# Moving layer 3's modulation slabs into layer 2's gated linear attention, with one pair of banks for the level planes

## What is computed

```python
for i in range(4):
    m_lat = (cond_lat @ mod_w[i] + mod_b[i]).reshape(1, 6, 1, 1024)     # and m_ctx alike
    h = x * (1 + m[1]) + m[0]
    y = mixer_i(h)                    # i == 2: bidirectional gated linear attention
    x = layer_norm(alpha * x + m[2] * y)
    h = x * (1 + m[4]) + m[3]
    x = layer_norm(alpha * x + m[5] * conv_ffn(h))
# the gated linear attention, per head and direction, in chunks of tokens:
#   o = q*exp(b) @ s + tril(sum_d q_i k_j exp(b_i - b_j)) @ v ;  s = s*exp(b_last) + (k*exp(b_last-b))^T v
```

## Time and profile before

| | |
|---|---|
| median of 3 runs | 2703.88 us (2703.25 to 2704.19) |
| the profiled execution's own time | 2701.32 us |
| its span, first to last instruction | 2699.5 us |
| mean granted TensorE clock, of 1 | 0.965 |
| TensorE matmuls busy | 2489.7 us (92%) |
| VectorE busy | 1499.6 us (56%) |
| ScalarE busy | 1172.0 us (43%) |
| GpSimd busy | 444.0 us (16%) |
| DMA | 310.43 MB, mean 115 GB/s |

### The profile page before, as it was taken

One profiled execution on the slowest core, in us unless ns is written; L12 is line 12 of the kernel. 1 busy time (PEld: TensorE's weight loads), 2 busy tenths in 40 slices (PEclk: granted clock), 3 DMA queues, 4 the chain that ended last, 5 costly groups with the idle time before them and its releaser, 6 DMA issues.

```text
span 2699.5 us, 37949 instructions
## 1 busy us (share of the span) xinstructions
PE 2489.7 (92%) x14922; PEld 2001.1 (74%) x14922; DVE 1499.6 (56%) x2244; ACT 1172.0 (43%) x2196; POOL 444.0 (16%) x443
## 2 busy tenths in 40 slices
PE   6999899999998899999999986788999999888997
PEld 3755877778888477777788875568777788856997
DVE  2465655553534857455434378867545434466874
ACT  3365533332422755333325344445333324256663
POOL 0000311110200012111012146623111002101111
PEclk8999999999999999999999997889999999999998
DMA  8602266653232013666433210013656434512663
GB/s 249 212 17 89 85 186 184 183 166 95 68 109 71 1 48 119 186 183 184 123 88 103 79 40 1 1 40 93 181 180 187 141 98 92 139 40 67 191 177 106
DMA packets 500561, 310.43 MB, mean 115 GB/s; under 512 B 24144, under 2 KB 499328, under 8 KB 500384
## 3 DMA queue, kind: packets, MB, share of 16 engines
q1 hardware_dynamic: 498048, 307.39, 38.8%
q10 hardware_dynamic: 2336, 0.61, 0.1%
HBM read 306.91 MB, written 1.05 MB: 114 GB/s over the span
## 4 chain that ended last, share of the span: by engine, by line
PE 79%; DVE 9%; ACT 5%; issue 4%; DMA 2%; POOL 0%; SPq 0%; ACTq 0%; DVEq 0%; POOLq 0%
PE bank L1463 69%; PE bank L1515 3%; PE bank L1642 1%; DMA slab_raw<-in_mod_w 1%; ACT p L641 1%; DVE stat L1105 1%; PE bank L1655 1%; PE bank L1683 1%; DMA slab_raw<-in_a_w_o 1%; DVE masked L1212 1%; DVE scores L1218 1%; DVE slab_lo L886 1%; ACT pt L653 1%; ACT slab_hi L460 1%; ACT hb L475 1%
## 5 line engine op out<-in xcount | busy, mean ns | idle before, releaser
L1463 PE MATMUL bank<-h_hi,slab_hi 128*128 128x512 f32 (+1 forms) x2416 | 857.6, 355 | 39.0 <-DVE slab_lo L886 26.0
L886 DVE TENSOR_TENSOR slab_lo<-slab_raw,slab_hi 128x1024 fp32r<-128x1024 f32 (+1 forms) x388 | 550.5, 1421 | 584.3 <-ACT slab_hi L460 583.2
L1463 PE MATMUL bank<-h_lo,slab_hi 128*128 128x512 f32 (+1 forms) x2416 | 835.1, 346 | 0.0
L1463 PE MATMUL bank<-h_hi,slab_lo 128*128 128x512 f32 (+1 forms) x2416 | 834.8, 346 | 0.0
L460 ACT ACTIVATE slab_hi<-slab_raw 128x1024 fp32r<-128x1024 f32 (+1 forms) x388 | 401.5, 1036 | 535.5 <-PE bank L1463 289.0
L1463 PEld LDWEIGHTS bank<-h_hi,slab_hi 128*128 128x128 f32 x2416 | 463.7, 192 | 147.1 <-issue 89.9
L1463 PEld LDWEIGHTS bank<-h_hi,slab_lo 128*128 128x128 f32 x2416 | 463.4, 192 | 55.7
L1463 PEld LDWEIGHTS bank<-h_lo,slab_hi 128*128 128x128 f32 x2416 | 464.1, 192 | 50.5 <-issue 0.8
L855 ACT ACTIVATE conv<-bank,prm 128x512 f32<-128x512 f32 (+1 forms) x176 | 127.2, 723 | 356.9 <-PE bank L1463 356.8
L1463 PE MATMUL bank<-g_hi,slab_hi 128*128 128x512 f32 (+1 forms) x770 | 269.3, 350 | 2.1 <-ACT res_t L511 2.1
L1463 PE MATMUL bank<-g_hi,slab_lo 128*128 128x512 f32 (+1 forms) x770 | 267.2, 347 | 0.0
(11 more groups left out here) (209 smaller groups left out, 3076.0 us busy)
## 6 DMA issues: line engine op xcount, KB each, us to landing
slab_raw<-in_mod_w SPq DMA_DIRECT2D x192, 512.0 KB, 4.6
slab_raw<-in_ffn_w_up SPq DMA_DIRECT2D x176, 512.0 KB, 4.7
slab_raw<-in_ffn_w_down SPq DMA_DIRECT2D x64, 512.0 KB, 3.8
slab_raw<-in_ffn_w_down SPq DMA_DIRECT2D x32, 384.0 KB, 3.4
slab_raw<-in_b_w_qkv SPq DMA_DIRECT2D x24, 512.0 KB, 3.7
slab_raw<-in_c_w_in SPq DMA_DIRECT2D x24, 512.0 KB, 3.8
slab_raw<-in_d_w_qkv SPq DMA_DIRECT2D x24, 512.0 KB, 6.6
slab_raw<-in_a_w_qkv SPq DMA_DIRECT2D x12, 512.0 KB, 5.6
```

The costliest lines, as they stand in the source:

```text
L886: nc.vector.tensor_tensor(wlo[slot][:, 0:w], raw[of][:, 0:w], whi[slot][:, 0:w].bitcast(f32), ALU.subtract).then_inc(s_lo, 1)
L1463: ins = mm(out, l, r, start=first and n == 0, stop=last and n == 2)
```

## The change

The 48 slabs of layer 3's modulation leave layer 2's up projection. In the list of loads they now stand behind the third slab of layer 2's output projection (`wo`), and on TensorE `mod_slab(5, m)` is called between `levels(c + 1)` and `chunk(c)`: one slab in even chunks, two in odd ones. They accumulate in bank 2, as bank 6 is in use there; for that, the level planes of all chunks use banks 0 and 1, and `levels(c)` waits for the masking of chunk c - 1. The row copy moves to the end of the attention on VectorE, ahead of the last head's gating, and the turn behind the first tile of the output projection.

```diff
 def mods_in_up(i, j, k, layers):
-    return [m for m in range(48) if 4 + m * (2 * FT - 4) // 48 == 2 * j + k] if i + 1 < layers else []
+    return [m for m in range(48) if 4 + m * (2 * FT - 4) // 48 == 2 * j + k] if i < 2 else []
+def mods_in_gla(c):
+    return range(48 * c // (2 * C_ITEMS), 48 * (c + 1) // (2 * C_ITEMS))
...
+            if i == 2 and dt == 2:
+                for m in range(48):
+                    order.append(("mod", len(mods)))
+                    mods.append(mod_items(5)[m])
...
+        def mod_bank(part):
+            return bank[2] if part == 5 else MOD_ACC
...
-                        ps = bank[2 * (c % 2) + h][:].rearrange("p (l i) -> p l i", l=4)
+                        ps = bank[h][:].rearrange("p (l i) -> p l i", l=4)
...
+                mod_row_copy(5)
                 head_gated(C_HEADS - 1)
                 head_lo(C_HEADS - 1)
...
-                    if c >= 2:
-                        pe.wait_ge(S["masked"], c - 1)
+                    if c:
+                        pe.wait_ge(S["masked"], c)
                     ks, qs = (right, left) if bwd else (left, right)
-                    out = bank[2 * (c % 2)]
+                    out = bank[0]
...
                     if c + 1 < n_chunks:
                         levels(c + 1)
+                    for m in mods_in_gla(c):
+                        mod_slab(5, m)
                     chunk(c)
...
+                if i == 2:
+                    pe.wait_ge(s_mod_row, 6)
                 for e in range(whole):
                     group_free(fg + e)
                     out_project(e, s_used)
+                    if i == 2 and e == 0:
+                        mod_turn(5)
...
-                    if dt == 0 and i + 1 < layers:
+                    if dt == 0 and i < 2:
                         mod_turn(i + 3)
```

More of the change, by code:

```diff
@@ L894, in mod_row_copy @@
                     dve.wait_ge(s_mod_t, part)
-                nc.vector.tensor_copy(mod_row[:], MOD_ACC[:]).then_inc(s_mod_row, 1)
+                nc.vector.tensor_copy(mod_row[:], mod_bank(part)[:]).then_inc(s_mod_row, 1)
             def mod_evacuate(i, g0, g1, part):
@@ L1345, in _ @@
                 round_rest(FT - 1)
-                if i + 1 < layers:
+                if i < 2:
                     mod_row_copy(i + 3)
@@ L1514, in mod_slab @@
                     z = cond_pad - 2 * g + TILE * (4 * q + j)
-                    ins = mm(MOD_ACC[TILE * j:TILE * j + TILE, NB // 2 * h:NB // 2 * h + NB // 2], cond_wide[:, z:z + TILE],
+                    ins = mm(mod_bank(part)[TILE * j:TILE * j + TILE, NB // 2 * h:NB // 2 * h + NB // 2], cond_wide[:, z:z + TILE],
                              raw[slot][:, NB // 2 * j:NB // 2 * j + NB // 2], start=g == g0 and q == 0,
@@ L1734, in levels @@
                         plane = l - 2
-                        out = bank[2 * (c % 2) + plane // 4][:, CH * (plane % 4):CH * (plane % 4) + CH]
+                        out = bank[plane // 4][:, CH * (plane % 4):CH * (plane % 4) + CH]
                         if l < LEVELS:
```

## The result

The changed kernel takes 2708.93 us, median of 14 runs, against 2703.43 us for 14 runs of the kernel before: the ratio is 1.002, 95% interval 1.0013 to 1.0027. It is 5.5 us slower, where 1.2 us faster was forecast. One execution of the 14 took 4837.12 us and was disturbed; the other 13 lie between 2704.01 and 2712.97 us. The profiled execution after took 2707.74 us, span 2705.9 us, mean granted clock 0.962.

What follows compares the result with a forecast made beforehand. TensorE was taken to bound the up projection, VectorE the attention; -35 + 33.8 = -1.2 us from the profiled 2701.32 gives 2700.1, and 2.56 to the median makes 2702.7 us, range 2687 to 2717.

Steps and rivals of the forecast that it cites:

- The up projection: Layer 2's up projection, bound by TensorE, gives back 35 us when the 48 slabs leave it.
- Row copy, turn, loads: Row copy while VectorE stands still, turn moved to the output projection, slab loads in the attention: zero net.
- The loop: Attention: masking, planes, slabs, outputs and update, state, masking become one loop; second chunks take 6.4 us against 4.62.
- The attention's sum: All chunks of the attention together lengthen by 33.8 us, between 23 and 50.
- first of a head (0, 8, 16, 24): These attention chunks take 5.5 us against 4.14, +1.35 each, 5.4 in all.
- fourth, 7, 15, 23: These attention chunks, where VectorE only waits for outputs, take 6.9 us against 4.65: +2.3 each, 6.9 in all.
- 3, 11, 19, 27 and what they delay (4, 12, 20, 28): In these attention chunks the delay reaches the next chunk's state: 8.2 us in all.
- the lower bound: Attention's price if TensorE's clock were high after 7 long waits: 1.6 us less each, 23 us in all.
- the prediction's own signs of being wrong: Attention: gated third chunks lengthen, planes behind long waits run in 2.2 us, or slabs cost other than 0.7 and 1.15.
- the terms written for chunk 11 and 12: Attention: masking at 1655.34 plus both chunks' work gives 1665.5 for a state that came at 1663.64, +2.0 us.
- the clock stays down: Rival, chance 0.18: in the attention half of 14 short loops run at the lower clock, 7 x 3.2 = 22 us: 2725.
- The clock comes up: Rival, chance 0.20: added TensorE work in the attention lifts the granted 0.82; 2691.7 us if all 7 restarts run high.

Runs made afterwards that it cites:

- experiment 3: The changed kernel with each chunk's modulation slabs ahead of the next chunk's planes and the wait for the masking: 2683.75 us, ratio 0.9938.
- experiment 8: The changed kernel with three plane banks, slabs in bank 3 ahead of the wait, two per third chunk, four per fourth: 2663.92 us, ratio 0.9851.
- Experiment 1: The kernel before with one shared pair of banks for the level planes, slabs left in the up projection: 2728.88 us, ratio 1.0091.
- experiment 4: The changed kernel with five idle matmuls ahead of the planes in chunks 3, 7, 15, 23 and 26: 2699.63 us, ratio 0.9988.
- 6: The changed kernel with three banks for the level planes and bank 3 for the slabs, still behind the planes: 2677.95 us, ratio 0.9902.
- 7: The changed kernel with three plane banks and bank 3 for the slabs, which stand ahead of the two waiting plane matmuls: 2677.71 us, ratio 0.9894.
- experiment 10: The kernel before with one shared pair of banks, plus one idle matmul in first and second chunks and 26, 30: 2719.64 us, ratio 1.0065.
- experiment 2: The changed kernel with slabs loaded but each used by one 32-column matmul, the row copy reading another bank: 2703.05 us, ratio 1.0004.

## Why the prediction was wrong

The direction was missed by a small sum of two large terms; the larger term of the loss was sized too low.

- **The up projection: right.** -35 forecast, 36.2 given back with the down projection, 0.8 of them the turn.
- **Row copy, turn, loads: right.** Nothing each, net, as the rows after show; experiments 3 and 8 clear the loads.
- **The loop: right in mechanism.** Experiment 1 shows the shared banks alone: 16.6 us more in the attention in its faster profile, 29.6 in its slower, +25.5 in the medians. Experiment 3 shows the slabs' place: 17.5 us over before with the slabs ahead of the wait, and the change another 25.3 above that, which makes the 42.75.
- **The attention's sum: wrong, 33.8 against 42.75.** By the chunk's place in its four, masking to masking:

| chunks | forecast | measured |
|---|---|---|
| second (1, 5, 13, 21, 29 and 9, 17, 25) | 10.5 | 9.0 |
| first of a head (0, 8, 16, 24) | 5.4 | 10.9 |
| third with a gate (2, 6, 10, 14, 18, 22) | 0 | 0 |
| 26 and 30 | 2.8 | 4.1 |
| fourth, 7, 15, 23 | 6.9 | 11.1 |
| 3, 11, 19, 27 and what they delay (4, 12, 20, 28) | 8.2 | 6.9 |
| 31 | 0 | 0.8 |

The step that failed is the price of the lower clock in two of these. For the fourth chunks the prediction has planes of 3.49 us, "the clock being at its lower level", and then 1.4 and 1.0 us for slabs and outputs, little above the full-clock prices. In chunk 7 after, from start to start, the planes take 3.81 us, the slabs 1.86 and the outputs 1.62 up to the copy (the lower level holds through the slabs and the first outputs): +3.8, 3.7 and 3.6 us in place of 2.3, and experiment 4 prices the lower clock there at 2.8 to 2.9 us where 1.6 stood in the lower bound. For the first chunks the loop of 5.5 us was reckoned "at the full clock", and they take 2.3 to 3.1 us more instead of 1.35. In 8, 16 and 24 the clock falls in the middle of the planes, behind a wait of 1.69 or 1.70 us: in chunk 8 the planes take 3.24 us and the slab 1.01 where 2.17 and 0.7 were reckoned. In chunk 0 it is already down when the planes begin (granted clock 0.50 from 1580 to 1586 us). These two rows are 5.5 + 4.2 = 9.7 us, more than the 9.0 by which the sum was short; the others together gave 0.7 back. For the fourth chunks this is shown by experiment 4; for the first ones it is read from the durations and the granted clock, and no run gave them filler alone.

One of the prediction's own signs of being wrong came true: slabs in the attention cost 1.9 and 1.0 us where the clock is low, not 1.15 and 0.7. And a sum in it is off: the terms written for chunk 11 and 12 add up to 1665.3 us, which is +1.7 and not +2.0; 1.4 was measured. The time itself lies inside the stated range; what was wrong is the direction.

The rival *the clock stays down* named the mechanism, but as a case of its own beside a sum without it: it counted 14 short loops, decided "from three such loops on" and put 3.2 us on each. In the profile after, the five second chunks are all at the full clock and it is the four first chunks of a head that fall; their price is 1.0 to 1.7 us beyond the forecast. Why these and not those is open: the second chunks have two slabs and the first ones one, but in experiment 4 a second chunk with two slabs fell too (chunk 5, 7.96 us). A partial rival should have been in the sum. And a forecast of -1.2 us out of terms of 35 and 34 us, each known to some microseconds, left the sign open: the time came out at the very bound of 0.2%, with an interval that lies wholly above no change.

*The clock comes up* did not happen (0.82 before and after). It did in other kernels: from 1576 to 1786 us the granted clock is 0.87 in kernel 3, 0.89 in 4, 0.89 in 6, 0.87 in 7 and 0.90 in 8. In 3, 4, 7 and 8 work stands ahead of a wait; 6 has the slabs behind the planes and only two planes behind the wait. The Trainium skill, page "TensorE: Matmul & The Clock Gate", section "What's actually happening", says that the default state is throttled and that activity releases it. By that rule work added in a wait can shorten what follows; experiments 4 and 10 agree (9.3 us less, and 9.2 us less than the median without filler), and experiment 2 shows its other side: with work taken away, three second chunks took 7.12 us where two others took 5.59.

Not tried: which chunks of the change fall to the lower level in its other executions. Its runs scatter by 9 us, and only one has a profile, so the table is of that one. The price of the lower clock in the first chunks in particular could be another in the next execution.

## What to carry to other kernels

Work meant for an engine's idle time fills it only if it stands in the queue ahead of the instruction that waits; behind it, it is added to the other engine's loop (25 us here for the same 48 slabs). A buffer freed by sharing is paid for with a wait, so look how much of the tile needs the shared part: two of six planes behind the wait cost nothing, six cost 25 us. And price a wait on TensorE by what comes after it as well, to the end of the loop and not for the first instructions alone: try filler in the long waits (9.3 us here), and allow for a short loop to run at the lower clock in some executions.

## What the hardware showed unexpectedly

- A short loop with a wait of 1.4 us has two durations in the same program, 5.15 and 6.79 us. With such loops the attention of one kernel took 220.20 us in one execution and 233.20 in another, at granted clocks of 0.82 and 0.75.
- The clock fell inside a group of matmuls with no wait in it: in chunk 8 of the change, L1740 took its full-clock 0.92 us and L1746, right behind it, 2.02 us where 1.16 is its full-clock time.
- Matmuls whose result is not used made two kernels faster, by 9.3 us (25 of them) and by 9.2 us (18), and removing 48 slabs' multiplications from the attention made it shorter by only 7.8 us (246.35 to 238.56).
